# Routing and gates by tile 76, up- and down-projection fused from tile 80 on, every down-projection tile in three products

## The chip, the cores and the metric

One core of a Trainium2 chip runs the whole step. The metric is the device time of one execution in microseconds; the kernel before stands at a median of 1876.55 us over 3 runs (1875.07 to 1878.01). The clock of TensorE is told as a share of 2.4 GHz, of which the records of this case show two levels, 1.0 and 0.5.

## The reference, cut to what matters

One encoder layer: attention of two kinds, then PEER, a retrieval of single-neuron experts, added to the residual, then a norm. The change lies wholly within PEER, which reads per token 16 experts for each of 8 heads out of 16,384:

```python
q = (xb @ w_q).reshape(tb, PEER_HEADS, 2, D_KEY // 2)
s = jnp.einsum('thpc,pnc->thpn', q, sub_keys)
s_top, i_top = lax.top_k(s, PEER_TOPK)
cand_s = (s_top[:, :, 0, :, None] + s_top[:, :, 1, None, :])...
best_s, best_j = lax.top_k(cand_s, PEER_TOPK)
gate = jax.nn.softmax(best_s, axis=-1)
pre = jnp.einsum('thkd,td->thk', u[expert], xb)
act = jax.nn.gelu(pre) * gate
return jnp.einsum('thk,thkd->td', act, v[expert])
```

There are 576 tokens of width 1024: 512 of a prompt and 64 of a sample.

## The kernel before, in words

The first 600 us are projections and attention, which the change does not touch. PEER then treats the tokens in two ways. For 384 tokens (blocks D0, D1, D2) it computes all experts: 128 up-projection tiles ("U tiles") of 128 experts each, Gelu, a multiplication with a matrix of gates that is zero where an expert wasn't chosen, and 128 down-projection tiles ("V tiles"). For the other 192 tokens (blocks A with 128 and B with 64) GpSimd (POOL) gathers the chosen rows of u and v, 512 KB at a time, into a ring of buffers, 5 of them and 7 later on; VectorE (DVE) makes 192 dot products from rows of u and 192 weighted sums from rows of v. `OPS` is their order, and the table `DOT_LINE` tells how many DVE does beside each U tile.

**U tiles** (lines 974 to 992 on PE). Weights come as f32 by SP's queue into 4 buffers (`load_u`). ScalarE (ACT) rounds them to a high part, DVE subtracts it (`lo_part`, line 1339), and PE makes 3 products of rounded parts, 24 matmuls of 384 columns. ACT applies Gelu; the result of 112 tiles is stored to memory and loaded again, that of the last 16 (`KEPT`) stays.

**Routing and gates.** DVE finds the chosen experts beside the U tiles in small steps (`PLAN`, and `STEP_LINE` for how many per tile). From tile 64 on (`G_AT`), for 48 tiles, each has two groups of one-hot matrices (line 1718), which ACT scales and PE multiplies ("scatters", line 969); the gate matrix goes to memory.

**V tiles** (lines 994 to 1015). PE takes them in 128 places, `V_TILES` saying which tile stands at which place. Three places in four (`SPLIT`) are done as three products of rounded parts, 18 matmuls of 512 columns: ACT rounds p and v, DVE subtracts (`p_low`, `v_low`). Each fourth place is done in plain f32 (line 1012). Ahead of each place DVE multiplies the activations with the gates (`product`, line 1787), in the order `v_low(i+1)`, `product(i+3)`, `p_low(i+2)`, then some gathered sums.

**SP's queue in this stage** is written out by hand and waits in order. At place i it waits for V tile buffer i+6 to be free, that is for place i to be done (6 buffers), and asks for the next V tile; at some places it then asks for 4 tiles of activations; and it asks for gates, which come in groups of `GL_TILES` = 16 tiles, 2 buffers, each group in 4 pieces at i % 16 = 0, 3, 6, 9. DVE's product of a group's first tile waits for all 4 pieces.

## Time and profile before

| | |
|---|---|
| median of 3 runs | 1876.55 us |
| the profiled execution: its time, its span | 1875.91 us, 1874.1 us |
| PE busy | 1777.3 us, 95% |
| DVE busy | 1434.5 us, 77% |
| ACT, POOL busy | 778.4 us, 644.6 us |
| moved by DMA | 478.22 MB, 255 GB/s over the span |
| mean granted clock | 0.973 |

In this table PE looks like the one bound. It is an average over stages, and the stages are read in the windows and the chain further down. Matmul records overlap, since PE pipelines, so what a tile costs is read from the chain of waits, where starts follow each other; likewise DVE's records overlap by some 0.08 us, and its prices are read from start to start.

### The profile page before, as it was taken

To read this page: it belongs to the slowest core of one execution; us is meant where nothing else is said; L and a number is where in the kernel's file an instruction comes from. 1 tells how busy PE (TensorE), PEld (TensorE's weight loads), DVE (VectorE), ACT (ScalarE), POOL (GpSimd) and SP (SyncE) were. 2 spreads that over 40 slices of the span, in tenths; PEclk is the share of its full clock that TensorE was granted. 3 is DMA by queue.
4 is the path that set the end of the run, shared out by engine and by line. 5 is a ranking of instruction groups with operands and counts; after the bars stand their busy time and mean duration, and the time that the engine had idled before them with its cause. 6 is when DMAs were issued, how large, how long until landed. Compare 5 with 4: busy or idle time off the path is not lost.

```text
span 1874.1 us, 26361 instructions
## 1 busy us (share of the span) xinstructions
PE 1777.3 (95%) x9675; PEld 1516.0 (81%) x9675; DVE 1434.5 (77%) x2750; ACT 778.4 (42%) x1555; POOL 644.6 (34%) x409
## 2 busy tenths in 40 slices
PE   6999999989999899999999999978999999999997
PEld 6999776559998899999899999976676666766764
DVE  4433676665678788989999999867888788888787
ACT  3112566553444333333768788522222222222222
POOL 1100000000000133434223366555557566665672
PEclk8999799789999999999999999999999999999998
DMA  6233100002222589989788899999999999999996
GB/s 217 68 131 121 45 1 1 1 1 85 68 77 95 185 305 334 316 307 327 262 276 297 279 387 387 386 400 333 386 389 382 401 387 389 401 402 384 400 379 216
DMA packets 153599, 478.22 MB, mean 255 GB/s; under 512 B 14896, under 2 KB 53808, under 8 KB 149888
## 3 DMA queue, kind: packets, MB, share of 16 engines
q1 hardware_dynamic: 96112, 264.62, 38.7%
q0 software_dynamic: 56928, 208.28, 30.4%
q10 hardware_dynamic: 432, 3.64, 0.5%
q8 instruction: 77, 1.26, 0.3%
q14 instruction: 50, 0.41, 0.1%
HBM read 419.47 MB, written 56.75 MB: 254 GB/s over the span
## 4 chain that ended last, share of the span: by engine, by line
PE 69%; DVE 16%; DMA 8%; ACT 3%; issue 3%; POOL 0%; SPq 0%; ACTq 0%; DVEq 0%
PE ps L1003 17%; PE ps L981 16%; PE ps L633 10%; PE ps L1012 7%; PE ps L918 5%; DMA g_in<-gates_scattered 4%; PE ps L723 3%; DVE hot L1718 3%; DVE w_lo L1339 3%; DVE ring L1737 2%; PE ps L969 2%; PE ps L714 2%; PE ps L766 2%; DMA ring<-u_rows,idx_b 1%; DMA raw<-w_tiles 1%
## 5 line engine op out<-in xcount | busy, mean ns | idle before, releaser
L981 PE MATMUL ps<-md_hi,w_hi 128*128 128x384 f32 x1024 | 358.6, 350 | 36.9 <-DVE w_lo L1339 36.7
L981 PE MATMUL ps<-md_hi,w_lo 128*128 128x384 f32 x1024 | 345.8, 338 | 0.0
L981 PE MATMUL ps<-md_lo,w_hi 128*128 128x384 f32 x1024 | 345.7, 338 | 0.0
L613 POOL DMA_INDIRECT ring<-u_rows,idx_a x128 | 197.2, 1541 | 404.2 <-DVE dots L1737 294.8
L1339 DVE TENSOR_TENSOR w_lo<-raw,w_hi 128x1024 fp32r<-128x1024 f32 x176 | 215.3, 1223 | 79.2 <-ACT w_hi L1265 59.4
L613 POOL DMA_INDIRECT ring<-v_rows,idx_a x128 | 225.1, 1759 | 136.7 <-DVE acc L1747 105.4
L1737 DVE CUSTOM_DVE_ANT_0 ring<-ring,x_n 128x1024 f32<-128x1024 f32 x192 | 230.7, 1223 | 12.7 <-DMA ring<-u_rows,idx_b 10.7
L1747 DVE SCALAR_TENSOR_TENSOR acc<-ring,actg,acc 128x1024 f32<-128x1024 f32 x188 | 234.8, 1282 | 0.0
L981 PEld LDWEIGHTS ps<-md_hi,w_hi 128*128 128x128 f32 x1024 | 194.5, 190 | 46.3 <-DVE w_lo L1339 45.3
L1003 PE MATMUL ps<-w_hi,p_hi 128*128 128x512 f32 x576 | 193.0, 416 | 9.4 <-DVE w_lo L1805 9.1
L981 PEld LDWEIGHTS ps<-md_lo,w_hi 128*128 128x128 f32 x1024 | 194.5, 190 | 0.0
L981 PEld LDWEIGHTS ps<-md_hi,w_lo 128*128 128x128 f32 x1024 | 194.0, 189 | 0.0
L1003 PE MATMUL ps<-w_hi,p_lo 128*128 128x512 f32 x576 | 182.3, 397 | 0.0
L1308 ACT CAST w_hi<-v_buf 128x1024 fp32r<-128x1024 f32 x96 | 100.4, 1046 | 196.9 <-PE ps L1003 190.5
L1805 DVE TENSOR_TENSOR w_lo<-v_buf,w_hi 128x1024 fp32r<-128x1024 f32 x96 | 117.5, 1224 | 83.9 <-ACT w_hi L1308 83.7
L1003 PE MATMUL ps<-w_lo,p_hi 128*128 128x512 f32 x576 | 180.6, 395 | 0.0
L633 PE MATMUL ps<-m_hi,w_hi 128*128 128x296 f32 (+1 forms) x496 | 152.4, 307 | 14.6 <-DVE w_lo L1339 14.6
L1012 PE MATMUL ps<-v_buf,act_in 128*128 128x512 f32 x360 | 159.3, 592 | 0.0
L633 PE MATMUL ps<-m_hi,w_lo 128*128 128x296 f32 (+1 forms) x496 | 150.4, 303 | 0.0
L633 PE MATMUL ps<-m_lo,w_hi 128*128 128x296 f32 (+1 forms) x496 | 149.9, 302 | 0.0
L1003 PEld LDWEIGHTS ps<-w_hi,p_hi 128*128 128x128 f32 x576 | 108.1, 189 | 51.2 <-issue 27.6
L1265 ACT CAST w_hi<-raw 128x1024 fp32r<-128x1024 f32 x127 | 132.3, 1042 | 22.5 <-DMA raw<-w_tiles 22.4
(265 smaller groups left out, 3261.2 us busy)
## 6 DMA issues: line engine op xcount, KB each, us to landing
raw<-w_tiles SPq DMA_DIRECT2D x176, 512.0 KB, 5.2
v_buf<-v_rows SPq DMA_DIRECT2D x128, 512.0 KB, 11.4
gates_scattered<-g_st SPq DMA_DIRECT2D x24, 1024.0 KB, 6.7
g_in<-gates_scattered SPq DMA_DIRECT2D x32, 768.0 KB, 15.8
activated<-act_st SPq DMA_DIRECT2D x112, 192.0 KB, 4.2
act_in<-activated SPq DMA_DIRECT2D x28, 768.0 KB, 12.9
kv_t<-qkv ACTq DMA_DIRECT2D x3, 1184.0 KB, 4.7
xh<-x_t SPq DMA_DIRECT2D x8, 296.0 KB, 6.0
```

Of the source, the lines that this page charges most:

```text
L613: pool.indirect_dma_start(ring[slot][:], None, u_rows if table == "u" else v_rows, bass.IndirectOffsetOnAxis(ap=idx, axis=0)).then_inc(gat ...
L633: mm = nc.tensor.matmul(ps[:, 2 * slot + h, 0:width], w[:, slot, kc, :], x[:, kc, c0:c0 + width], start=(m == 0), stop=(m == 23))
L918: mm = nc.tensor.matmul(ps[:, 2 * slot + h, 0:HQ], w[:, slot, kc, :], x[:, kc, h * HQ:(h + 1) * HQ], start=(kc == 0 and j == 0), stop=(kc ...
L981: mm = nc.tensor.matmul(ps[:, slot, 0:ND], w[:, slot, kc, :], x[:, kc, :], start=(kc == 0 and j == 0), stop=(kc == KC - 1 and j == 2))
L1003: mm = nc.tensor.matmul(ps[:, 2 + 2 * t + h, :], p[:, q % 3, t * P:(t + 1) * P], v[q % 2][:, 512 * h:512 * h + 512], start=(i == 0 and n = ...
L1012: mm = nc.tensor.matmul(ps[:, 2 + 2 * t + h, :], acts(i)[:, t * P:(t + 1) * P], v_buf[i % V_SLOTS][:, 512 * h:512 * h + 512], start=False, ...
L1265: nc.scalar.copy(w_hi[:, n % 2], raw_u[k]).then_inc(hi_ready, 1)
L1308: nc.scalar.copy(v_hi[q % 2], v_buf[i % V_SLOTS][:]).then_inc(v_hi_ready, 1)
L1339: TT(w_lo[:, slot], raw[:, slot] if src is None else src, w_hi[:, slot].bitcast(F32), SUB).then_inc(w_split, 1)
L1737: nc.vector.tensor_tensor_reduce(rows, rows, x_n[:, blk], 1.0, 0.0, MULT, ADD, dots[:, blk, k:k + 1]).then_inc(gath_used, 1)
L1747: nc.vector.scalar_tensor_tensor(dst, rows, by, dst, MULT, ADD).then_inc(gath_used, 1)
L1805: TT(v_lo[q % 2], v_buf[i % V_SLOTS][:], v_hi[q % 2].bitcast(F32), SUB).then_inc(v_ready, 1)
```

## The change

1. **Routing earlier.** Blocks D0, D1, D2 are routed ahead of B (`PLAN`, with `RANK` for the count of finished blocks), all by tile 72. Gates are made beside tiles 28 to 75 (`G_AT` 28).
2. **Gathers moved.** `OP_LINE` takes the place of `DOT_LINE`: 25 gathered operations by tile 28, 45 by 76, 55 by 80, 252 by the end of U tile 127, the other 132 over the 80 V places behind. 16 sums of block A stand ahead of those of B.
3. **Fused part.** `FUSED` = 80: from U tile 81 on, each U tile is followed on PE by one V place, 47 places beside U tiles 81 to 127 and the rest behind ("the tail", places 47 to 127). The fused places take V tiles 80 to 127, whose activations stay on the core; 80 tiles are stored. The fused places have 4 buffers for V and one pair for its two parts (`vf_hi`, `vf_lo`), so the rounding of a V tile waits for the place before.
4. **Every V place split** (`SPLIT` is all 128).
5. **Gates in groups of 8 tiles**, pieces of 384 KB at j % 8 = 0, 2, 4, 6 instead of 768 KB at 0, 3, 6, 9 of 16.

The diff, cut to its core ("..." marks what is left out):

```diff
-PLAN = [("top", RT_A), ("sel", RT_B), ("top", RT_B), ("top", RT_D0), ("top", RT_D1), ("sel", RT_D2), ("top", RT_D2)]
+PLAN = [("top", RT_A), ("top", RT_D0), ("top", RT_D1), ("sel", RT_D2), ("top", RT_D2), ("sel", RT_B), ("top", RT_B)]
-STEP_LINE = [(0, 0), (7, 13), (64, 54), (90, N_STEPS)]
-G_AT = 64
+STEP_LINE = [(0, 0), (7, 13), (24, 26), (40, 39), (56, 57), (72, N_STEPS)]
+G_AT = 28
-GL_TILES = 16
-DOT_LINE = [(10, 0), (64, 67), (90, 97), (112, 140), (N_EXP, 178)]
+GL_TILES = 8
+FUSED = 80
+N_FUSED = N_EXP - FUSED
+V_TILES = [*range(FUSED, N_EXP), *range(FUSED)]
+OP_LINE = [(10, 0), (28, 25), (76, 45), (FUSED, 55), (N_EXP, 252), (N_EXP + FUSED, 384)]
...
-SPLIT = [i for i in range(N_EXP) if i % 4 != 3]
+SPLIT = list(range(N_EXP))
+V_SLOT, V_LAND, V_PREV = [], [], []
+for place in range(N_EXP):
+    slot = place % 4 if place < N_FUSED else (place - N_FUSED) % V_SLOTS
+    V_LAND.append(16 * (V_SLOT.count(slot) + 1))
+    V_PREV.append(max((p for p in range(place) if V_SLOT[p] == slot), default=None))
+    V_SLOT.append(slot)
...
+            def load_v(j):
+                slot, t = V_SLOT[j], V_TILES[j]
+                if V_PREV[j] is not None:
+                    sp.wait_ge(v_done, V_PREV[j] + 1)
...
+            def beside_place(j):
+                last = min(j + 3, N_FUSED - 1) if j < N_FUSED - 1 else min(j + V_SLOTS, N_EXP - 1)
+                while len(v_asked) <= last:
+                    load_v(len(v_asked))
+                    v_asked.append(j)
...
+                if j >= N_FUSED and j % 4 == 0:
+                    sp.wait_ge(v_done, j)
+                    g = (j - N_FUSED) // 4 + 2
+                    for g in range(1 if j == N_FUSED else g, min(g + 1, FUSED // 4)):
+                        load_acts(g)
+                if j >= 0 and j % 2 == 0 and 2 <= j // GL_TILES + 1 < N_EXP // GL_TILES:
+                    sp.wait_ge(p_made, j // GL_TILES * GL_TILES)
+                    load_gates(j // GL_TILES + 1, j % GL_TILES // 2)
...
-                if i % 16 in (0, 3, 6, 9) and i < N_EXP - 16:
-                    if i >= 16:
-                        sp.wait_ge(p_made, i // 16 * 16)
-                    load_gates(i // 16 + 1, i % 16 // 3)
+                if i > FUSED:
+                    beside_place(i - FUSED - 1)
+
+            for i in range(N_FUSED - 1, N_EXP):
+                beside_place(i)
...
+                if i == FUSED:
+                    pe.wait_ge(g_evac, N_GRP)
+                if i > FUSED:
+                    down(i - FUSED - 1)
+
+            for i in range(N_FUSED - 1, N_EXP):
+                down(i)
...
+                    q = SPLIT.index(i)
+                    act.wait_ge(v_in[V_SLOT[i]], V_LAND[i])
+                    before = q - (1 if i < N_FUSED else 2)
+                    if before >= 0 and (SPLIT[before] >= N_FUSED or i < N_FUSED):
+                        act.wait_ge(v_done, SPLIT[before] + 1)
...
             steps = routing()
             for i in range(N_EXP):
+                if i > FUSED:
+                    product(i - FUSED - 1)
...
+                if i > FUSED:
+                    p_low(i - FUSED - 1)
+                    v_low(i - FUSED - 1)
+                for s in ops_of(i):
                     gathered(s)
```

`down` holds the same 18 matmuls as the V loop before. In the tail DVE's order stays `v_low(i+1)`, `product(i+3)`, `p_low(i+2)`, sums.

How instructions stand on two engines, with the semaphores that they wait for (`v_done` counts finished places, `p_made` products, `g_in0` and `g_in1` landed gate pieces). First SP in the middle of the down-projection, before: the end of one group's pieces, with the requests for V tiles 90 to 95 (the last `g_in` row stands at place 89).

```order
L490 DMA v_buf_139<-v_rows 128x1024 [waits v_done]
L480 DMA act_in_147<-activated 128x1536 [waits v_done]
L490 DMA v_buf_140<-v_rows 128x1024 [waits v_done]
L490 DMA v_buf_141<-v_rows 128x1024 [waits v_done]
L475 DMA g_in_145<-gates_scattered 128x6x256 [waits p_made]
L490 DMA v_buf_142<-v_rows 128x1024 [waits v_done]
L490 DMA v_buf_143<-v_rows 128x1024 [waits v_done]
L480 DMA act_in_148<-activated 128x1536 [waits v_done]
L490 DMA v_buf_144<-v_rows 128x1024 [waits v_done]
L475 DMA g_in_145<-gates_scattered 128x6x256 [waits p_made]
```

After, in the tail, the end of a group of 8 (V tiles 87 to 92; the last `g_in` row stands at place 86, after the request for V tile 92).

```order
L507 DMA v_buf_144<-v_rows 128x1024 [waits v_done]
L507 DMA v_buf_145<-v_rows 128x1024 [waits v_done]
L491 DMA g_in_148<-gates_scattered 128x6x128 [waits p_made]
L507 DMA v_buf_146<-v_rows 128x1024 [waits v_done]
L507 DMA v_buf_141<-v_rows 128x1024 [waits v_done]
L496 DMA act_in_151<-activated 128x1536 [waits v_done]
L491 DMA g_in_148<-gates_scattered 128x6x128 [waits p_made]
L507 DMA v_buf_142<-v_rows 128x1024 [waits v_done]
L507 DMA v_buf_143<-v_rows 128x1024 [waits v_done]
L491 DMA g_in_148<-gates_scattered 128x6x128 [waits p_made]
```

Before, the last piece stands at place 89 and product 96 is the first that needs it; now it stands at place 86, and product 88 is the first that needs it.

DVE where a new group of gates begins, before: `act_in` rows are products, the one that waits for `g_in0` is product 96; there is no `p_lo` behind it for place 95, which is an f32 place.

```order
L1805 TENSOR_TENSOR w_lo<-v_buf_143,w_hi 128x1024 [waits v_done,v_hi_ready]
L1787 TENSOR_TENSOR act_in_148<-act_in_148,g_in_145 128x384 [waits act_in1,g_in0]
L1747 SCALAR_TENSOR_TENSOR acc<-ring_95,actg,acc 128x1024 [waits gath_used,gath_in2]
L1747 SCALAR_TENSOR_TENSOR acc<-ring_96,actg,acc 128x1024 [waits gath_used,gath_in3]
L1787 TENSOR_TENSOR act_in_148<-act_in_148,g_in_145 128x384
L1796 TENSOR_TENSOR p_lo<-act_in_148,p_hi 128x384 [waits v_done,p_hi_ready]
L1747 SCALAR_TENSOR_TENSOR acc<-ring_97,actg,acc 128x1024 [waits gath_used,gath_in4]
L1805 TENSOR_TENSOR w_lo<-v_buf_139,w_hi 128x1024 [waits v_done,v_hi_ready]
```

After, the same for product 88, which waits for `g_in1`; the `p_lo` behind it is that of place 87.

```order
L1794 SCALAR_TENSOR_TENSOR acc<-ring_97,actg,acc 128x1024 [waits gath_used,gath_in4]
L1801 TENSOR_TENSOR acc<-acc,b_half 64x1024 [waits b_sum,b_folded]
L1845 TENSOR_TENSOR w_lo<-v_buf_143,w_hi 128x1024 [waits v_done,v_hi_ready]
L1822 TENSOR_TENSOR act_in_150<-act_in_150,g_in_148 128x384 [waits act_in1,g_in1]
L1834 TENSOR_TENSOR p_lo<-act_in_149,p_hi 128x384 [waits v_done,p_hi_ready]
L1794 SCALAR_TENSOR_TENSOR acc<-ring_98,actg,acc 128x1024 [waits gath_used,gath_in5]
L1845 TENSOR_TENSOR w_lo<-v_buf_144,w_hi 128x1024 [waits v_done,v_hi_ready]
```

Between product 88 and `v_low` of place 87 (the last row) stand the remainder of place 87's p and one sum; PE's place 87 needs both remainders.

DVE in one iteration at the end of the U tiles, before (`dots` rows without a source finish the row ahead):

```order
L1339 TENSOR_TENSOR w_lo<-raw,w_hi 128x1024 [waits hi_ready]
L1737 ISA ring_97,dots<-ring_97,x_n 128x1024 [waits gath_in4]
L1737 ISA dots 128x1
L1737 ISA ring_93,dots<-ring_93,x_n 128x1024 [waits gath_in0]
L1737 ISA dots 128x1
L1339 TENSOR_TENSOR w_lo<-raw_100,w_hi 128x1024 [waits hi_ready]
```

After, one fused iteration:

```order
L1822 TENSOR_TENSOR act_in_150<-act_in_150,g_in_148 128x384 [waits act_done]
L1385 TENSOR_TENSOR w_lo<-raw_100,w_hi 128x1024 [waits hi_ready]
L1834 TENSOR_TENSOR p_lo<-act_in_150,p_hi 128x384 [waits v_done,p_hi_ready]
L1845 TENSOR_TENSOR vf_lo<-v_buf_141,vf_hi 128x1024 [waits v_done,v_hi_ready]
L1783 ISA ring_97,dots<-ring_97,x_n 128x1024 [waits gath_in4]
L1783 ISA dots 128x1
L1783 ISA ring_93,dots<-ring_93,x_n 128x1024 [waits gath_in0]
L1783 ISA dots 128x1
L1783 ISA ring_94,dots<-ring_94,x_n 128x1024 [waits gath_in1]
L1783 ISA dots 128x1
L1783 ISA ring_95,dots<-ring_95,x_n 128x1024 [waits gath_in2]
L1783 ISA dots 128x1
```

The product of a place, its two remainders and some four gathered operations now stand between two weight remainders of U tiles, where two or three gathered operations stood.

## Rows read from the trace of the kernel before

**Rows 1.** The page's slices, forty of the span: busy tenths of PE and DMA.
```profile
PE   6999999989999899999999999978999999999997
DMA  6233100002222589989788899999999999999996
```
**Rows 2.** Windows: stretch, length, busy us (instructions) of engines, PEclk, DMA share, GB/s.
```profile
888.00:1058.00 170.00, 160.15 (x1039) 157.05 (x1038) 165.53 (x317) 123.95 (x306) 52.94 (x31) 0.99 0.84 284
1058.00:1191.00 133.00, 129.80 (x864) 129.12 (x864) 128.21 (x160) 108.00 (x268) 77.21 (x43) 1.00 0.97 364
1191.00:1286.00 95.00, 77.09 (x431) 74.02 (x429) 69.56 (x102) 30.84 (x50) 52.48 (x41) 0.97 0.99 376
1286.00:1860.00 574.00, 570.88 (x2112) 398.35 (x2112) 463.70 (x542) 143.76 (x194) 347.11 (x202) 1.00 1.00 380
```
**Rows 3.** The chain that ended last: start us, us, what.
```profile
609.41 4.17 PE ps L981 x24
...
1097.85 2.63 PE ps L981 x15
1103.85 2.63 PE ps L981 x15
...
1306.17 12.56 PE ps L1003 x54
1318.73 5.15 PE ps L1012 x12
...
1860.40 3.68 DVE h_fin L1850 x6
```
**Rows 4.** DVE's timeline in the gate stage: start us, us, instruction.
```profile
1099.09 2.36 DVE L1718 TENSOR_TENSOR hot<-cst,rt_t 128x1024 f32<-128x1024 f32 x2
1101.36 1.23 DVE L1339 TENSOR_TENSOR w_lo<-raw,w_hi 128x1024 fp32r<-128x1024 f32 x1
1102.50 1.23 DVE L1737 CUSTOM_DVE_ANT_0 ring<-ring,x_n 128x1024 f32<-128x1024 f32 x1
1103.64 0.09 DVE L1737 DVE_READ_ACCUMULATOR2_ANT dots<- 128x1 f32 x1
```
**Rows 5.** DVE's timeline in the down-projection; in brackets idle time and its releaser.
```profile
1481.40 1.22 DVE L1805 TENSOR_TENSOR w_lo<-v_buf,w_hi 128x1024 fp32r<-128x1024 f32 x1
1482.54 0.55 DVE L1787 TENSOR_TENSOR act_in<-act_in,g_in 128x384 f32<-128x384 f32 x1
1483.01 0.55 DVE L1796 TENSOR_TENSOR p_lo<-act_in,p_hi 128x384 fp32r<-128x384 f32 x1
1483.48 2.47 DVE L1747 SCALAR_TENSOR_TENSOR acc<-ring,actg,acc 128x1024 f32<-128x1024 f32 x2
...
1494.91 0.56 DVE L1787 TENSOR_TENSOR act_in<-act_in,g_in 128x384 f32<-128x384 f32 x1 [5.19 <-DMA g_in<-gates_scattered]
```
**Rows 6.** Windows of line 981 alone, the U tiles: PE and weight loads, clock, DMA.
```profile
592.00:733.00 141.00, 119.93 (x659) 115.20 (x660) 0.99 0.73 250
```
**Rows 7.** Groups by line: ACT's rounding of a V tile.
```profile
L1308 ACT CAST w_hi<-v_buf 128x1024 fp32r<-128x1024 f32 x96 | 100.4, 1046 | 196.9 <-PE ps L1003 190.5 <-DMA v_buf<-v_rows 6.4
```
**Rows 8.** SP's timeline in the down-projection.
```profile
1473.84 0.33 SPq L490 DMA_DIRECT2D v_buf<-v_rows  x1
1474.22 0.43 SPq L475 DMA_DIRECT2D g_in<-gates_scattered  x1
```
**Rows 9.** DVE's waits from 1286 to 1860: us in total, times, longest.
```profile
DVE act_in L1787 <- DMA g_in<-gates_scattered: 26.0, 6, 6.0
```
**Rows 10.** PE's timeline at the first V tiles.
```profile
1285.88 1.19 PE L1003 MATMUL ps<-w_hi,p_hi 128*128 128x512 f32 x2 [6.28 <-DVE w_lo L1805]
...
1291.08 0.64 PE L1003 MATMUL ps<-w_hi,p_hi 128*128 128x512 f32 x2
```
**Rows 11.** The tile g_in: its loads of 768 KB.
```profile
DMA to landing us min/median/max: 7.6/15.8/21.5
```
**Rows 12.** The tile v_buf: its loads of 512 KB.
```profile
DMA to landing us min/median/max: 4.0/11.4/20.3
```

More of the change, by code:

```diff
@@ L525, in _ @@
                                  g_st[:, b % 2].rearrange("p i t -> p (i t)")).then_inc(g_stored[b % 2], 16)
+                if i == G_END + 1:
+                    for j in range(4):
+                        load_v(j)
+                        v_asked.append(j)
                 if i == G_END + 2:
@@ L971, in scatter, with down @@
                 mm.then_inc(hot_used, 1)
+            def down(i):
+                if i in SPLIT:
+                    q = SPLIT.index(i)
+                    hi, lo = v_parts(i)
+                    pe.wait_ge(p_ready, q + 1)
+                    pe.wait_ge(v_ready, q + 1)
+                    for t in range(3):
+                        for n, (p, v) in enumerate(((p_hi, hi), (p_hi, lo), (p_lo, hi))):
+                            for h in range(2):
+                                mm = nc.tensor.matmul(ps[:, 2 + 2 * t + h, :], p[:, q % 3, t * P:(t + 1) * P],
+                                                      v[:, 512 * h:512 * h + 512],
+                                                      start=(i == 0 and n == 0), stop=(i == N_EXP - 1 and n == 2))
+                    mm.then_inc(v_done, 1)
+                    return
+                pe.wait_ge(p_made, i + 1)
+                pe.wait_ge(v_in[V_SLOT[i]], V_LAND[i])
+                for t in range(3):
+                    for h in range(2):
+                        mm = nc.tensor.matmul(ps[:, 2 + 2 * t + h, :], acts(i)[:, t * P:(t + 1) * P],
+                                              v_buf[V_SLOT[i]][:, 512 * h:512 * h + 512],
+                                              start=False, stop=(i == N_EXP - 1))
+                mm.then_inc(v_done, 1)
             for i in range(N_EXP):
@@ L1741, in gathered @@
                 if s == N_U:
-                    dve.wait_ge(v_done, KEPT // 2)
+                    for stored in g_stored:
+                        dve.wait_ge(stored, 16 * (N_GB // 2))
                 if k < 2:
@@ L1802, in v_low @@
                     dve.wait_ge(v_hi_ready, q + 1)
-                    if q >= 2:
-                        dve.wait_ge(v_done, SPLIT[q - 2] + 1)
-                    TT(v_lo[q % 2], v_buf[i % V_SLOTS][:], v_hi[q % 2].bitcast(F32), SUB).then_inc(v_ready, 1)
-            product(0)
-            product(1)
-            product(2)
-            p_low(0)
-            v_low(0)
-            p_low(1)
-            for i in range(N_EXP):
+                    before = q - (1 if i < N_FUSED else 2)
+                    if before >= 0:
+                        dve.wait_ge(v_done, SPLIT[before] + 1)
+                    hi, lo = v_parts(i)
+                    TT(lo[:], v_buf[V_SLOT[i]][:], hi[:].bitcast(F32), SUB).then_inc(v_ready, 1)
+            steps = routing()
+            for i in range(N_EXP):
+                if i > FUSED:
+                    product(i - FUSED - 1)
+                for g in groups_of(i, 0):
+                    one_hot(g)
+                if i + 1 < N_EXP:
+                    lo_part(B_U + i + 1, (i + 1) % 2, raw_u[(i + 1) % RAW_SLOTS])
+                for s in range(5):
+                    if i == GATE_TILE[s] + 1:
+                        gates_of(s)
+                if i == OP_LINE[0][0] - 2:
+                    normed_rows()
+                for _ in range(along(STEP_LINE, i), along(STEP_LINE, i + 1)):
+                    s = next(steps)
+                    if s is not None:
+                        assert GATE_TILE[s] == i, (s, i)
+                        gates_below(s)
+                if i > FUSED:
+                    p_low(i - FUSED - 1)
+                    v_low(i - FUSED - 1)
+                for s in ops_of(i):
+                    gathered(s)
+            product(N_FUSED - 1)
+            p_low(N_FUSED - 1)
+            v_low(N_FUSED - 1)
+            for j in range(3):
+                product(N_FUSED + j)
+            p_low(N_FUSED)
+            v_low(N_FUSED)
+            p_low(N_FUSED + 1)
+            for i in range(N_FUSED, N_EXP):
                 if i + 1 < N_EXP:
@@ L1819, in _ @@
                     p_low(i + 2)
[L1820 removed]
+                for s in ops_of(N_EXP + i - N_FUSED):
                     gathered(s)
[L1822 to L1828 removed]
             n_fin = 0
```

242 lines of the change are left out of this document (98 added, 144 removed).

## The prediction, made blind

> **What bounds the kernel now.** First view, the page's slices [rows 1]: PE stands at 9 in most of the forty, and the DMA digits reach 9 for good in the 24th, at 1078 us. Two resources are full at once, so the stages have to be read one by one. The windows by stage [rows 2] show which: from 888 to 1191 us the stage of the gates, DMA share 0.84 and then 0.97; from 1191 to 1286 the last up-projection tiles, where PE is busy for only 77 of 95 us and the DMA share is 0.99; from 1286 to 1860 the down-projection, PE busy 571 of 574 us and a DMA share of 1.00 at 380 GB/s. PE sets the time nearly everywhere, and the DMA engines have nothing left after 1191.
>
> The chain of waits gives PE's prices [rows 3]: an up-projection tile is 4.17 us; with two scatters beside it the tiles come every 6.00 us (1097.85 to 1103.85); three split down-projection tiles take 12.56, so one 4.19; one tile in plain f32 takes 5.15; after PE's last product 14 us remain (1860.40 to the end of the span). DVE's prices are read from one start to the next [rows 4, 5]: 1.14 for a rounding remainder of a weight tile, 2.27 for a pair of one-hots, 1.14 for a gathered dot product, 1.2 for a gathered sum, 0.47 each for a product with the gates and its remainder.
>
> **The gate stage moves forward.** The gates now cover tiles 28 to 75 instead of 64 to 111. At 733 us PE has done 659/24 = 27.5 tiles [rows 6], with much the same mix of routing and gathers as the new order has there, so tile 28 begins near 735. The 48 tiles took 303 us before (888 to 1191), since 31 gathers and 20 routing steps beside the first 26 of them kept DVE busy 165.5 of 170 us [rows 2]. From that window a routing step is worth (165.5 - 26 x 3.41 - 31 x 1.14)/20 = 2.1 us. After: 48 x 3.41 + 20 gathers x 1.14 + 45 steps x 2.1 = 281 us of DVE under 48 x 6.00 = 288 us of PE. PE covers it, barely; I take 290, so 1025 us at tile 76. Then five plain tiles with 2.5 gathers each, and the first gate pieces and V tiles queued behind them: 4.5 us each (4.17 if PE alone counts), 1047 us.
>
> **Fused rounds, 47 of them (tiles 81 to 127 with places 0 to 46).** PE: 4.17 + 4.19 = 8.36 us. DVE: two remainders 2.28, product and its remainder 0.94, and 197 gathers over 48 rounds, 4.1 x 1.15 = 4.7; sum 7.9. DMA: 512 KB for the U tile, 512 KB for V, 4.1 x 512 KB of gathers, 192 KB of gates: 3.39 MB, at the 380 GB/s of the saturated stage 8.9 us. So DMA sets the round. Below it is bounded by PE, 8.36; above by the gather rate of the saturated stage with the same ring of 5 buffers, 41 gathers in 95 us [rows 2], 4.1 x 2.32 = 9.5. I take 9.1, near the bytes: 428 us, place 46 done at 1475 us (bounds 393 and 447).
>
> What hides the new single-buffered split of V (vf_hi, vf_lo): the rounding may begin only when the place before is done, and one U tile of 4.17 us lies between, against 1.05 on ACT [rows 7] and 1.14 on DVE.
>
> **All tiles split.** 32 tiles go from 5.15 to 4.19: 31 us less on PE. The 32 added remainders cost DVE 32 x 1.61 = 52 us, which fits: a tail place has 1.14 + 0.94 + 1.65 x 1.2 = 4.06 us of DVE under 4.19. Fewer stored activations (80 tiles for 112) take 12.6 MB off the queues.
>
> **Where the change adds a wait: the last gate piece of each group.** This decides the forecast. SP asks for V tile j+6 only when place j is done, since six buffers are all it has, and the gate pieces stand behind that request on the same queue. Before, the last of four pieces of a group of 16 goes out after place 9 of 16 and is wanted for place 16. The trace shows what this slack was worth: issue at 1474.22 [rows 8], wanted by DVE at 1489.7, used at 1494.91 after 5.19 us of waiting [rows 5]; six such waits, 26 us in all [rows 9]. PE had places 10 to 15 to do meanwhile, and place 15 was an f32 tile that needs no remainder. Now groups have 8 tiles, and the last piece goes out at place 8k+6, after that place is done. DVE meets product 8k+8 before the remainder of p for place 8k+7, so PE has nothing to do from the end of place 8k+6 until the piece has landed. Queued behind that product on DVE are the gathered sums too, whose buffers POOL needs for its next gathers; ACT's roundings of p for 8k+8 and of V for 8k+7 wait with it. The slack went from six places to none.
>
> Its price: 0.4 us for the V request and the issue ahead [rows 8]; the landing; then on DVE product 0.47, remainder 0.47, one or two gathered sums 2.0, remainder of V 1.14, with PE's own start about 4.2; and half speed afterwards. That last one is seen once: after 6.28 us of idling PE's records of two products last 1.19 us at 1285.88 and 0.64 from 1291.08 on [rows 10]; half of those 5.2 us is lost, 2.6. The landing of such a piece took 7.6 to 21.5 us at twice the size [rows 11], and a V tile 4.0 at best [rows 12]. The 15.8 of the median belongs to a queue without gaps. In the tail a group needs 8 x (512 + 1.65 x 512 + 192 of gates + 192 of activations) KB = 14.3 MB, 37.5 us at 380 GB/s, and the hole makes the group last longer than that, so the queue has run nearly dry when the piece goes out. I take 7 us, near the shortest row. A boundary costs 0.4 + 7 + 4.2 + 2.6 = 14.2 us; with a landing of 4 it is 11.2, with 12 it is 19.2.
>
> In the fused rounds the same piece has a U tile and a place more in front of it, and DVE comes to the product only 4.19 + 1.05 + 1.14 + 4.7 = 11 us after the issue (the place, the split of the next V tile, the gathers). There I charge nothing beyond the 9.1.
>
> **The sum**, against the profiled execution's 1875.91 us (span 1874.1; the median of the runs is 1876.55, so 0.6 above): place 46 at 1475, place 47 at 1479. Product 48 waits for a piece issued when U tile 127 was done, 1471, into a full queue: 1471 + 0.4 + 15.8 + 4.2 + 2.6 = 1494. Then 80 places x 4.19 = 335 and nine boundaries (products 56 to 120) x 14.2 = 128: 1957. With 14 at the end 1971, and 1.8 outside the span: **1972 us**. Seen as differences: 13 won in the gate stage, 26 where PE idled from 1191 to 1286, 31 from f32; lost 35 on fused rounds above PE's price and 143 at group boundaries.
>
> **Rivals.** (a) The other side: the gate piece is not waited for at the boundaries. That would hold if SP ran a few places ahead, or if a piece landed in the time that DVE has work; it decides where a boundary costs under (1876 - 1494 - 335 - 16)/9 = 3.4 us. Then the bytes set the tail: 80 x 4.69 = 375 us at 380 GB/s, 356 at 400: 1479 + 356 to 375 + 16 = 1851 to 1870, faster by 0.3 to 1.3%. For it: DVE's whole wait for gates was 26 us before. Against: the order of SP's and DVE's instructions, which leaves no place between. (b) Empty queues: the piece lands in about 4 us and a boundary costs 11.2; 1972 - 27 = 1945, and with rounds at PE's price 1910. For it: the hole itself empties the queues. (c) Rounds bound by the ring of 5 and boundaries with 12 us of landing: 1972 + 19 + 45 = 2036. For it: landings of 12 us and more are the rule once several requests are out. That the change doesn't do what it says is ruled out: the order shows the fused places and the split tiles.
> The shortest landing of a gate piece in the trace is 7.6 us for 768 KB [rows 11]. [...]
>
> **How the numbers follow.** Forecast 0.52, (b) 0.28, (c) 0.12, (a) 0.08. The range from 1900 to 2035 holds the forecast and (b) with the bounds of the rounds, and (c) but for its end; (a) lies outside. Chances, with 0.2% as about what a measurement of this kernel can tell from no change: faster 0.06, same 0.02 (both from (a)), slower 0.92.
>
> **What would show it.** After: gate stage near 6.0 us per tile from tile 28; rounds of 8.9 to 9.5 us with a DMA share near 1; then in the tail a PE gap of 9 to 15 us every eight places, ended by a wait of DVE for g_in, with half the granted clock behind it, and a DMA share falling to about 0.8. If those gaps are missing, the step on the last gate piece is wrong, and (a) holds. If the gaps are there but the rounds take over 10 us, the gather ring was mis-sized.

## The result: 2021.5 us, 7.8% slower, and the profile after

The changed kernel took 2021.53 us (median of four runs, 2015.98 to 2026.01) against 1875.81 for the kernel before, run beside it: a ratio of 1.0778, with a 95% interval from 1.0758 to 1.0798. The forecast was 1972 in a range from 1900 to 2035. The profiled execution took 2015.98 us with a span of 2014.2.

The page's slices of the changed kernel, to be laid beside [rows 1]. PE's nines end with the 30th slice, at 1511 us, in which the last U tile is done (1495.86); from there on PE and the DMA engines are both short of full, where before both were full.

```profile
PE   6999998899999989998995999999986776777756
PEclk9999798889999999999997999999998888888878
DMA  5243000012225887675779999999998888878885
```

The windows by stage, as in [rows 2]: stretch, length, busy us (instructions) of PE, weight loads, DVE, ACT and POOL, granted clock, DMA share, GB/s. They are the gate stage (tiles 28 to 75), the way to place 0, the fused rounds, the passage to places alone, and the tail with eight group boundaries.

```profile
748.00:1051.00 303.00, 292.06 (x1925) 287.52 (x1924) 271.05 (x545) 236.29 (x579) 34.52 (x21) 1.00 0.69 233
1051.00:1095.00 44.00, 23.10 (x124) 22.52 (x123) 23.02 (x33) 10.04 (x14) 16.25 (x14) 0.81 1.02 357
1095.00:1496.00 401.00, 388.64 (x1933) 349.62 (x1933) 371.75 (x507) 131.07 (x183) 256.30 (x188) 0.99 1.01 381
1496.00:1560.00 64.00, 41.68 (x163) 33.09 (x161) 36.19 (x43) 14.06 (x20) 22.00 (x16) 0.84 0.87 310
1560.00:1960.00 400.00, 279.69 (x1153) 227.16 (x1154) 264.85 (x302) 93.74 (x128) 184.55 (x107) 0.85 0.82 292
```

The tail is where the time went: PE works for 280 of 400 us. The waits of the whole span (us in total, times, longest) give the chain of causes: DVE waits for gate pieces where it waited 26.0 us before [rows 9], and PE waits for DVE's remainders behind that.

```profile
DVE act_in L1822 <- DMA g_in<-gates_scattered: 146.2, 10, 21.6
PE ps L1013 <- DVE w_lo L1845: 137.9, 12, 20.9
PE ps L1013 <- DVE vf_lo L1845: 33.9, 13, 16.8
```

One boundary in full, before place 87, from the timelines of SP, DVE and PE (start us, us, instruction, in brackets the idle time ahead and its releaser). They answer [rows 8], [rows 5] and [rows 10].

```profile
1745.59 0.33 SPq L507 DMA_DIRECT2D v_buf<-v_rows  x1
1745.97 0.43 SPq L491 DMA_DIRECT2D g_in<-gates_scattered  x1
...
1739.85 1.20 DVE L1845 TENSOR_TENSOR w_lo<-v_buf,w_hi 128x1024 fp32r<-128x1024 f32 x1
1754.95 0.56 DVE L1822 TENSOR_TENSOR act_in<-act_in,g_in 128x384 f32<-128x384 f32 x1 [13.90 <-DMA g_in<-gates_scattered]
1755.43 0.55 DVE L1834 TENSOR_TENSOR p_lo<-act_in,p_hi 128x384 fp32r<-128x384 f32 x1
1755.90 1.28 DVE L1794 SCALAR_TENSOR_TENSOR acc<-ring,actg,acc 128x1024 f32<-128x1024 f32 x1
1757.10 1.22 DVE L1845 TENSOR_TENSOR w_lo<-v_buf,w_hi 128x1024 fp32r<-128x1024 f32 x1
...
1744.95 0.61 PE L1013 MATMUL ps<-w_hi,p_lo 128*128 128x512 f32 x2
1758.46 1.19 PE L1013 MATMUL ps<-w_hi,p_hi 128*128 128x512 f32 x2 [12.90 <-DVE w_lo L1845]
1759.45 1.05 PE L1013 MATMUL ps<-w_lo,p_hi 128*128 128x512 f32 x2
...
1764.55 0.63 PE L1013 MATMUL ps<-w_lo,p_hi 128*128 128x512 f32 x2
```

This is the step of the prediction as it was drawn: the last matmuls of place 86 start at 1744.95, only then does SP ask for the next V tile and the last gate piece, DVE stands for 13.9 us, and PE starts 12.9 us later, for the first 6 us at a granted clock of 0.50 (two matmuls last 1.05 to 1.19 us instead of 0.62). There are nine such gaps, ahead of places 55, 63 and so on to 119, of 10.8 to 20.9 us.

The stretch around it in windows, 1720 to 1768, shows something that the prediction had wrong: the queue has not run dry when the last piece goes out. The DMA engines are full (share 1.03 and 1.04) at 1745.97 and for six us more. Cut to single us, their share is 1.09 from 1751 to 1752, then 0.64, 0.10 and 0.03; the piece lands at 1754.93. So they run empty only over the last 2 to 3 us of its way, and then idle while DVE and PE start again and have yet to free the buffers for new requests.

```profile
1720.00:1730.00 10.00, 10.00 (x45) 8.26 (x44) 10.00 (x12) 4.41 (x6) 8.01 (x4) 1.00 1.03 389
1730.00:1740.00 10.00, 10.00 (x46) 8.26 (x44) 10.00 (x12) 2.93 (x4) 6.40 (x6) 1.00 1.04 393
1740.00:1750.00 10.00, 4.73 (x20) 3.30 (x18) 1.05 (x1) 0.00 (x0) 1.88 (x1) 1.00 1.04 393
1750.00:1757.00 7.00, 0.00 (x0) 0.00 (x0) 2.04 (x3) 1.45 (x2) 0.00 (x0) 0.56 0.41 134
1757.00:1768.00 11.00, 9.54 (x30) 7.64 (x31) 9.88 (x12) 2.93 (x5) 8.05 (x5) 0.66 0.40 117
```

Counted over each of the eight groups from the packet records, the 14.2 to 16.5 MB of a group keep the 16 engines busy for 39 to 48 us, and they are idle for 9 to 12 (median 9.9) of its 49.95 us. So two things stand behind a group's time, PE's gap and the transfers, and the experiments had to tell how much belongs to each. (The packets' times overlap a little, which is why a share can be above 1.)

### The profile page after: what moved, and what is told of

Read it like the earlier page. It is cut to its first block, busy times and chain, and to the rows that moved or that the text cites. A ratio compares the mean times of both kernels' runs of the same rounds, so it can differ in the third digit from the quotient of the medians.

```text
span 2014.2 us, 27049 instructions
## 1 busy us (share of the span) xinstructions
PE 1760.2 (87%) x9867; PEld 1566.4 (78%) x9867; DVE 1491.8 (74%) x2814; ACT 821.0 (41%) x1619; POOL 598.6 (30%) x409
## 4 chain that ended last, share of the span: by engine, by line
PE 49%; DVE 23%; DMA 14%; issue 7%; ACT 3%; POOL 2%; SPq 2%; DVEq 0%; ACTq 0%
PE ps L1013 15%; PE ps L663 10%; PE ps L1035 7%; PE ps L948 5%; DMA g_in<-gates_scattered 4%; DVE w_lo L1385 3%; DVE ring L1783 3%; PE ps L753 3%; DMA ring<-u_rows,idx_b 3%; DMA ring<-u_rows,idx_a 3%; DVE acc L1794 3%; POOL ring L643 2%; DVE hot L1764 2%; PE ps L999 2%; PE ps L744 2%
## 5 line engine op out<-in xcount | busy, mean ns | idle before, releaser
L643 POOL DMA_INDIRECT ring<-u_rows,idx_a x128 | 180.8, 1412 | 504.9 <-DVE dots L1783 388.6
L1277 ACT CAST p_hi<-act_in 128x384 fp32r<-128x384 f32 x128 | 65.8, 514 | 571.1 <-DVE act_in L1822 398.7
L643 POOL DMA_INDIRECT ring<-v_rows,idx_a x128 | 218.4, 1707 | 231.1 <-DVE acc L1794 205.4
L1013 PE MATMUL ps<-w_hi,p_hi 128*128 128x512 f32 x480 | 158.1, 412 | 137.9 <-DVE w_lo L1845 137.9
L1013 PEld LDWEIGHTS ps<-w_hi,p_hi 128*128 128x128 f32 x480 | 94.5, 200 | 161.9 <-issue 142.6
L1822 DVE TENSOR_TENSOR act_in<-act_in,g_in 128x384 f32<-128x384 f32 x128 | 70.5, 552 | 153.7 <-DMA g_in<-gates_scattered 146.2
L1013 PE MATMUL ps<-w_lo,p_hi 128*128 128x512 f32 x480 | 154.3, 404 | 0.0
L1013 PE MATMUL ps<-w_hi,p_lo 128*128 128x512 f32 x480 | 153.4, 402 | 0.0
L1306 ACT ACTIVATE hot<-hot,rt_t 128x128 f32<-128x128 f32 x384 | 117.6, 391 | 28.3 <-DVE hot L1764 28.3
```

The costliest lines, as they stand in the source:

```text
L643: pool.indirect_dma_start(ring[slot][:], None, u_rows if table == "u" else v_rows, bass.IndirectOffsetOnAxis(ap=idx, axis=0)).then_inc(gat ...
L1013: mm = nc.tensor.matmul(ps[:, 2 + 2 * t + h, :], p[:, q % 3, t * P:(t + 1) * P], v[:, 512 * h:512 * h + 512], start=(i == 0 and n == 0), s ...
L1277: nc.scalar.copy(p_hi[:, q % 3], acts(i)).then_inc(p_hi_ready, 1)
L1306: last = nc.scalar.mul(h, h, rt_t[:, 2, 4 * g + t:4 * g + t + 1])
L1822: TT(p, p, g_in[grp % 2][:, :, V_TILES[i] % GL_TILES, :], MULT).then_inc(p_made, 1)
```

## The experiments

The ratios are to the kernel before, run beside each version (its medians were 1875.8 to 1879.7 us), with 95% intervals; medians in us.

| run | median | ratio | interval |
|---|---|---|---|
| changed kernel | 2021.5 | 1.0778 | 1.0758 to 1.0798 |
| last piece one place earlier | 2015.0 | 1.0737 | 1.0711 to 1.0763 |
| last piece three places earlier | 1956.5 | 1.0417 | 1.0393 to 1.0440 |
| product one place later on DVE | 2008.1 | 1.0689 | 1.0660 to 1.0717 |
| last piece seven places earlier | 1916.3 | 1.0184 | 1.0148 to 1.0220 |
| the same, fewer bytes | 1883.7 | 1.0012 | 0.9986 to 1.0038 |
| both starts | 2021.4 | 1.0759 | 1.0721 to 1.0797 |
| seven places earlier, both starts | 1908.5 | 1.0142 | 1.0108 to 1.0175 |
| long rows in the changed kernel | 2014.6 | 1.0728 | 1.0695 to 1.0761 |
| seven earlier, starts, long rows | 1892.1 | 1.0072 | 1.0046 to 1.0098 |
| before, all tiles split | 1887.3 | 1.0051 | 1.0031 to 1.0072 |
| before, long rows | 1869.7 | 0.9969 | 0.9950 to 0.9988 |
| before, all tiles split, long rows | 1863.5 | 0.9933 | 0.9913 to 0.9953 |

**The last gate piece one place earlier.** After the fused rounds, `at` names the places of a group behind which SP issues the four pieces ("..." marks what is left out):

```diff
-                if j >= 0 and j % 2 == 0 and 2 <= j // GL_TILES + 1 < N_EXP // GL_TILES:
...
+                at = (0, 2, 4, 6) if j < N_FUSED else (0, 2, 4, 5)
+                if j >= 0 and 2 <= j // GL_TILES + 1 < N_EXP // GL_TILES:
+                    for piece in range(4):
+                        if at[piece] == j % GL_TILES:
...
```

> The changed kernel with one line of SP's order altered: after the fused rounds the four gate pieces of a group go out after places 8k, 8k+2, 8k+4 and 8k+5, so the last one 4.1 us (one place) earlier than after place 8k+6. Theory (the wait at a group boundary is the time from the issue of the last piece to its landing): each of the nine PE gaps of 10.8 to 20.9 us gets shorter by one place, 4.1 us, and the stretch at half clock stays, since the gaps stay above 6 us: 9 x 4.1 = 37 us less than 2021, so about 1985. Rival (the DMA engines are at their limit in this stage and the late piece only shows it): a piece issued earlier lands as much later, the gaps stay, 2015 to 2022.

Measured: 2015.0, some 7 us less instead of 37. The intervals of the two ratios overlap, so the gain is at the edge of what can be told. The rows name the reason. The last piece ahead of place 87 goes out at 1742.57, and DVE goes on at 1755.16; in the changed kernel these stood at 1745.97 and 1754.95.

```profile
1738.11 0.33 SPq L507 DMA_DIRECT2D v_buf<-v_rows  x1
1738.48 0.50 SPq L496 DMA_DIRECT2D act_in<-activated  x1
1739.02 0.43 SPq L491 DMA_DIRECT2D g_in<-gates_scattered  x1
1742.19 0.33 SPq L507 DMA_DIRECT2D v_buf<-v_rows  x1
1742.57 0.44 SPq L491 DMA_DIRECT2D g_in<-gates_scattered  x1
...
1755.16 0.56 DVE L1826 TENSOR_TENSOR act_in<-act_in,g_in 128x384 f32<-128x384 f32 x1 [12.37 <-DMA g_in<-gates_scattered]
```

Its landing took 12.6 us instead of 9.0: the 768 KB of activations, the V tiles and the piece before were still in the queue. The two traces are shifted against each other; counted from the end of the gap before (1711.21 here, 1709.94 there) the piece was asked for 4.7 us earlier and DVE went on 1.1 us earlier, and a group takes 49.0 us for 49.95. So most of what the earlier issue won was lost again in the queue. Over one place the rival holds.

**Three places earlier.** `(0, 1, 2, 3)` in the same line.

> The same line altered further: pieces after places 8k, 8k+1, 8k+2 and 8k+3, the last one 12.3 us earlier than in the changed kernel. Theory: gaps of 10.8 to 16.8 us shrink to 0 to 4.5, too short for half clock behind them, so some 130 of the 149 us that the boundaries cost go, unless the bytes of the stage take over as the limit: a group of 8 places moves 14.3 MB, 37.5 us at the 380 GB/s of the old down-projection, so the 80 places could not take less than 375 instead of 487 us. Together 1885 to 1915. Rival (DMA at its limit already): 2000 to 2020, and a third story (the half clock comes from something else than the gaps) leaves the stretches at 0.500 in place, near 1960.

Measured: 1956.5, 65 us less, half of what the first theory gave and far more than the rival. The gaps are 2.1 to 11.3 us, half clock still behind most of them. The pieces land in 10.3 to 14.2 us in the stretch from 1741 to 1771, so part of the earlier issue is again eaten by the queue; but the queue now has work in time in which it was idle before (the DMA engines' idle time in a group is 4.4 us in the median for 9.9). Both stories were wrong by half. The third story named nearly this time, but not for its reason: of the eight gaps the seven of 7.4 us and more have half clock behind them, the one of 2.1 us has none, and in the version with the pieces seven places earlier, below, the long stretches at half clock go together with the gaps (granted clock 0.97). That gaps of up to 4.5 us would be too short for it is not borne out: in the changed kernel a gap of 4.75 us ahead of place 47 has 3.4 us at half clock behind it.

**The product one place later.** No transfer is moved; DVE makes the product two places ahead instead of three and the gathered sums ahead of the remainder of p, and ACT rounds V ahead of p, so place 87 no longer needs what stands behind product 88. DVE's part of the edit:

```diff
-                if i + 3 < N_EXP:
-                    product(i + 3)
-                if i + 2 < N_EXP:
-                    p_low(i + 2)
+                if N_EXP > i + 2 > N_FUSED + 2:
+                    product(i + 2)
                 for s in ops_of(N_EXP + i - N_FUSED):
                     gathered(s)
+                if i + 2 < N_EXP:
+                    p_low(i + 2)
```

> The changed kernel with no transfer issued at another time; after the fused rounds DVE makes the product with the gates two places ahead instead of three, behind the remainder of V of the next place, and ACT rounds V before p. So the first product of a group no longer stands ahead of what place 8k+7 needs, and PE has that place to do while the last gate piece is on its way. Theory: as much as one place's earlier issue, 4.1 us at each of nine boundaries, 37 in all: about 1985. Rival (the order of DVE's instructions doesn't matter, PE would wait for the same landing anyhow and the place is only moved to the other side of the gap; or the products made later delay the places in between): 2015 to 2030.

Measured: 2008.1, 13 us less, with intervals that don't touch. So the order on DVE is a part of the cause, as the prediction said; a group takes 48.6 us from the end of one gap to the end of the next (1567.9 to 1956.4, eight groups) instead of 49.95, 1.4 less where a place is 4.1. The DMA share stays at 0.84 and the pieces land later again, in 9 to 23 us.

**The theory after these three.** In a group of 8 places PE and the transfers each have work for less than the group takes, but each waits for the other once: the transfers' work (some 39 us) and the idle time that the boundary gives them (10 us) make up the group. An earlier issue can win the idle time and no more. That was put to the test with the piece seven places earlier, and with fewer bytes.

**Seven places earlier.** From the group of products 64 on, the pieces go out after places 8k-4 to 8k-1:

```diff
+  first = (g - 1) * GL_TILES
+  at = [first + 2 * n for n in range(4)] if first < N_FUSED else [
+      max(first - 4, N_FUSED) + n for n in range(4)]
...
```

> The changed kernel with the four gate pieces of a group issued after places 8k-4, 8k-3, 8k-2 and 8k-1 from the group of products 64 on (the group of 56 after places 48 to 51): the last one seven places, 28 us, earlier than in the changed kernel. Theory as now amended (PE's places and the transfers run one after the other: the DMA engines are at their full rate for 39 us of each group of 8 places and idle for 10 to 12 beside PE's gap; an earlier issue can win the idle time only): no wait for gate pieces is left, the group takes the 39 us that its 14.2 MB take at 370 to 380 GB/s, against 49.5 in the changed kernel and 43.2 with the last piece three places earlier: the time falls by 10 x 3.7 from 1956, to about 1920 (1905 to 1930), with a DMA share near 1. The prediction's own sum, with nothing but PE's 4.19 a place behind the gaps: 8 x 4.19 = 33.5 a group, 1956 - 97 = 1860. Rival (the queue holds what is asked for earlier just as long): 1950 to 1960.

Measured: 1916.3. DVE waits for no gate piece after the fused rounds, the gaps from place 55 to 119 are at most 4.0 us long, and what is left there is the transfers' limit. The window from place 55 to 119 of this kernel, to be laid beside the changed kernel's window from 1560 to 1960 above:

```profile
1558.00:1852.00 294.00, 273.26 (x1152) 219.75 (x1150) 262.92 (x298) 95.79 (x128) 190.22 (x105) 0.97 1.04 390
```

64 places in 294 us, 36.8 a group, DMA share 1.04, idle time of the DMA engines 0.0 in every group, 4.6 us a place where PE needs 4.1. The prediction's rival (a) had this price: 4.45 to 4.69 us a place once no piece is waited for.

**Fewer bytes.** The same with the loads of stored activations left out from the fourth group of four places on.

```diff
-                        load_acts(g)
+                        if g < 3:
+                            load_acts(g)
...
```

> The same with 17 of the 20 loads of stored activations left out, so the products from the fourth group of four places on are made from the wrong activations: a group of 8 places moves 12.6 MB instead of 14.2, 34.7 us of the DMA engines' time instead of 39. Theory (bytes set the places once no piece is late): 10 groups x 4.3 = about 40 us below the run with the early pieces, near 1880. Rival (PE, DVE or the order of the waits sets them): within 10 us of it.

Measured: 1883.7, 33 us less; a group takes 33.0 us (264/8), which is PE's 8 x 4.12.

```profile
1551.00:1815.00 264.00, 262.60 (x1155) 216.18 (x1154) 262.99 (x301) 94.00 (x129) 199.85 (x106) 1.00 1.04 385
```

So with all bytes the transfers set the places. With 11% fewer PE does, with 262.6 of 264 us busy, but only just: the DMA share is still 1.04. The loads left out also take their own waits away, but those were 5.6 us of DVE's in the version before, too little for the 33. The amended theory stands: 1920 and 1880 were expected.

**Both starts.** One V tile instead of four ahead of the first gate pieces, the pieces of group 1 after places 0, 2, 4 and 6, and another order of V buffers at place 48:

```diff
-    slot = place % 4 if place < N_FUSED else (place - N_FUSED) % V_SLOTS
+    slot = place % 4 if place < N_FUSED else (place - N_FUSED + 4) % V_SLOTS
...
-                    for j in range(4):
-                        load_v(j)
-                        v_asked.append(j)
+                    load_v(0)
+                    v_asked.append(0)
...
```

> The changed kernel with its group boundaries as they are, and the two starts mended: at tiles 77 to 79 SP asks for one V tile, the gate pieces of group 0 and one more V tile, the pieces of group 1 follow after places 0, 2, 4 and 6 (instead of four V tiles and both groups' pieces before place 0); and places 48 and 49 use the two V buffers that come free with the last U tile, not those of places 44 and 45. Theory: group 0's pieces had 1.5 MB of group 1's and 2 MB of V tiles in the queue beside them, and landed 17 to 24 us after their issue; without them the PE gap of 16.8 us before place 0 shrinks to 5 to 9 us, and the gap of 6.9 us before place 51 goes, with half clock behind each: 12 to 22 us less, 2000 to 2010. Rival (the gap before place 0 is the scattered gates' own way through memory, which no order changes): only the second, 2012 to 2016.

Measured: 2021.4 in the median, so nothing that can be told from no change, though its profiled execution took 2007.85. In the trace the gap ahead of place 0 is 11.4 us for 16.8, and the one ahead of place 51 is 4.1 for 6.9; with the early pieces beside it the latter is 7.0. The second half of the expectation is wrong. What DVE waits for ahead of place 51 is a group of activations (7.51 us in the changed kernel, 4.79 here): behind place 47 the changed kernel asks for four V tiles, two groups of activations and a gate piece within 7 us, 4.1 MB, and the order of the buffers makes them no fewer.

**Seven places earlier and both starts.**

> The early pieces and both starts together. Theory: the savings are at different places and add up, if the bytes leave room: 1920 less 12 to 22, about 1900 to 1908. If the stage after the fused rounds is set by its bytes, what the second start wins is given back there, and it is 1908 to 1915. Rival (the time lost at the starts is filled with transfers that then fail to stand in the queue later, so nothing is won): 1920.

Measured: 1908.5, on the border of the two ranges expected, but its interval overlaps that of the early pieces alone; whether the starts add anything stays open.

**Long rows.** The gates lie in DRAM by groups of 8 tiles, so a row of a piece has 3 KB instead of 512 bytes.

```diff
-    sp.dma_start(g_in[buf][:, b0:b0 + N_GB // 4].rearrange("p b i t -> p b (i t)"),
-                 g_dram[b0 * P:(b0 + N_GB // 4) * P, tiles * n:(tiles + 1) * n].rearrange(
-                     "(b p) n -> p b n", p=P)).then_inc(g_in_s[buf], 16)
+    sp.dma_start(g_in[buf][:, b0:b0 + N_GB // 4].rearrange("p b i t -> p (b i t)"),
+                 g_dram[tiles * P:(tiles + 1) * P, b0 * n:(b0 + N_GB // 4) * n]).then_inc(g_in_s[buf], 16)
...
```

> The changed kernel with one thing altered: the scattered gates lie in DRAM by groups of 8 tiles, so a gate piece has rows of 3 KB instead of 512 bytes (and the 24 stores of the gate stage have rows of 512 bytes instead of 8 KB). Theory (the transfers' time counts, and half a tile group per piece made it longer: 49152 packets of 512 bytes took 30 ns each in the changed kernel, 92 us over the 16 engines; the same bytes in 3 KB packets would take some 125 ns each by the rows of 1.5 and 4 KB, 64 us): 1.75 us less for each of 16 groups, of which the ten behind the fused rounds count in full since PE's work and the transfers follow one another there: 17 to 28 us less, 1993 to 2004. The stores' longer time is covered, since the DMA share of the gate stage is 0.68. Rival (the gaps are set by order alone, and the bytes are the same): 2016 to 2022.

Measured: 2014.6, 7 us less, where 17 to 28 were expected; the intervals of the two ratios overlap, so this too is at the edge of what can be told. The transfers did get shorter, by 1.3 to 2.5 us in each group, but the DMA engines' idle time grew from 10 to 11 us: as long as the gap is there, it is the order that sets it, and a shorter transfer is worth what it takes off the landing of the last piece (median of all pieces 8.5 us for 9.2).

> Early pieces, both starts and the long rows together. Theory: the stage behind the fused rounds is all transfer time now (idle time of the DMA engines 0.0 in each group), so the packets' 1.75 us a group come off in full there and in part in the fused rounds: 1908 less 17 to 28, 1880 to 1891, level with the kernel before or a little above it. Rival: PE or the waits set the places, 1903 to 1908.

Measured: 1892.1, 16 us less than without the long rows, with intervals that don't touch, and a microsecond above the expected range. Where the transfers set the places the shorter packets count. All parts of the changed kernel's loss that were tried are mended in this version, and it is still 0.7% slower than the kernel before. Its trace still has gaps of 10.3 us ahead of place 0, 5.0 us ahead of place 51 and 10.1 us near the end; what else it lacks stays open.

**The split alone, and the kernel before with long rows.** In the kernel before, one line (and the stop flag of the last place):

```diff
-SPLIT = [i for i in range(N_EXP) if i % 4 != 3]
+SPLIT = list(range(N_EXP))
```

> The kernel before with one part of the change alone: all 128 tiles of the down-projection as three products of rounded parts, instead of 96 of them. Theory of the prediction: PE is given back 32 x (5.15 - 4.19) = 31 us, and DVE's 52 us more fit beside it; if PE set the stage of 574 us alone that gives 1845. But the DMA share of that stage is 1.00, so the bytes set it nearly as tightly: then the gain is 0 to 12 us, 1864 to 1876, with PE gaps in place of the plain tiles. A third way: each group now lacks the plain tile that needed no remainder, so the wait for gate pieces reaches PE: slower by up to 20 us, 1895.

> The kernel before with the long rows alone (6 KB rows in a gate piece instead of 1 KB, stores with rows of 1 KB). Its gate pieces took 24576 x 48 ns / 16 = 74 us, by the packets of 6 KB (240 ns) it would be 61: 12 us of transfers less in a stage of 574 us whose DMA share is 1.00. But PE is busy there for 571 us: theory (both limits lie within a per cent of one another), 1870 to 1877. Rival (the bytes alone set that stage): 1865.

> The kernel before with two things: all tiles of the down-projection split, and the long rows. Theory (the split's 31 us were not to be had since the transfers set the stage; they come to light as far as the transfers get shorter): 12 us below the run with the split alone, 1887 - 12 = 1875, and some more where gaps with half clock behind them go: 1862 to 1875, below the kernel before. Rival (the split alone was slower because of the missing plain tile at each group's end, not because of the transfers): 1880 to 1887.

Measured: 1887.3, 1869.7 and 1863.5. The long rows alone are worth 0.3%, at the lower edge of the theory's 1870 to 1877. The split alone makes the kernel before 0.5% slower. PE's busy time falls (549 us, for 571 in [rows 2]), but the stage gets longer, from 574 to 584 us. Its gate pieces are waited for again, now by PE as well, with half clock behind: the third way of the expectation. The rows, of DVE and of PE:

```profile
1638.83 0.56 DVE L1787 TENSOR_TENSOR act_in<-act_in,g_in 128x384 f32<-128x384 f32 x1 [8.44 <-DMA g_in<-gates_scattered]
...
1643.53 1.20 PE L1003 MATMUL ps<-w_hi,p_hi 128*128 128x512 f32 x2 [7.64 <-DVE w_lo L1805]
```

The long rows bring the landing of a piece from 15.0 us in the median to 11.9 (15.8 in the kernel before [rows 11]), and with them the split wins: in the window of that stage PE is busy 541.6 of 554 us at a DMA share of 1.00.

```profile
1286.00:1840.00 554.00, 541.61 (x2303) 432.99 (x2301) 515.94 (x605) 186.25 (x255) 349.62 (x201) 0.99 1.00 394
```

That version is faster than both kernels, by 0.7% than the one before (0.9913 to 0.9953). The rival (the missing plain tile, not the transfers) falls in so far as the pieces now come in time without that tile.

## Why the prediction was right, step by step

The direction, the mechanism and its place were right, and the sum came out 50 us short (1972 for 2021.5; 44 against the profiled execution). In order of time:

- **Gate stage, 290 us for 48 tiles: wrong, 303.6.** ACT's Gelu of tile 28 is at 747.76 and that of tile 76 at 1051.40. The same 48 tiles took 303 before as well [rows 2]. The step priced a tile at the 6.00 us of one row of the chain [rows 3]; PE's busy time per tile in the stage is 292/48 = 6.08, and 0.2 of idling comes on top. DVE was not the limit (271 of 303 us), as said. With a start that lay some 9 us later than 735 (a Gelu comes a tile of PE after that tile's start), this is 22 us.
- **The way to place 0: a term that was missing, about 20 us.** PE idled 16.8 us ahead of place 0, with half clock behind. The first four gate pieces were issued at 1060.68 into a queue with four V tiles and U tiles ahead of them and landed after 10 to 24 us. The prediction had "the first gate pieces and V tiles queued behind them" and gave them 0.3 us a tile.
- **Rounds of 9.1 us: 8.72.** 46 of them from 1094.66 to 1495.86. The DMA share is 1.01, and the round lies inside its bounds (8.36 to 9.5), nearer to PE's price than the forecast. That gives 18 back. No product waits for gates there, as said.
- **Product 48 waits 15 us for its piece: it did not.** The piece landed in 5.7 us, and places 47 and 48 start at 1504.9 and 1510.68. That gives 8 back, after a gap of 4.75 us ahead of place 47 with half clock behind it. Ahead of place 51 stands a gap of 6.87 us instead: DVE waits 7.51 us for a group of activations that is asked for at 1515.33, behind four V tiles, and lands 9.9 us later. The sum had no term for it; with half clock it cost some 10.
- **A place, 4.19: 4.08.** Over 80 places 9 us less.
- **A boundary, 14.2 us, nine of them: 16.6, 149 for 128.** Taken apart at place 87: V request 0.4, landing from the issue on 9.0 (7 taken), DVE and PE's start 3.5 (4.2 taken), half clock 3.0, and 1.4 to 3.0 over the nine (2.6 taken). The landing was the size that was off: the nine last pieces took 6.8 to 14.6 us, 9.4 in the mean, and 2.4 us more at each of nine boundaries are the 21. Its reason was wrong: "the queue has run nearly dry when the piece goes out". It was full then, and at place 87 for six us more. The last boundary cost 22.4, since the five loads of h_fin are issued at place 116 and the piece behind them takes 14.6 us.
- **31 us from f32 on PE: right for PE, and worth nothing.** The split alone cost the kernel before 10 us; no run takes it out of the changed kernel. The stage before was bound by PE and by the transfers at once, which the first part of the prediction saw ("the DMA engines have nothing left after 1191"), and the sum then took PE's part as if it came off alone.
- **The tail's price behind the boundaries.** The sum had 4.19 a place, PE's. With the boundaries mended it is 4.6, the transfers' (rival (a)'s price), so removing the wait gave 105 us and not 149.

Four terms were too low, by 22, 20, 10 and 21 us, and three too high, by 18, 8 and 9. That is 38 of the 44 us; 2 more lie behind PE's last product (16 for 14), and some 4 stay unplaced. So the mechanism was right, but that the time fell into the stated range is in part luck: errors of opposite sign, in a range 135 us wide. The list of differences at the end of the prediction's sum doesn't close either: 70 won and 178 lost make 108, where 1972 less 1876 is 96.

Of the rivals, (b) with a landing of 4 us and (a) with none to wait for fall by the rows above; the pieces in the tail landed in 6.8 to 18.4 us. (c) came nearest in time, with 2036, but its rounds of 9.5 us were too long, and the mean landing of 9.4 lies halfway between the 7 of the forecast and its 12. The Trainium skill (DMA: Bandwidth & Descriptors, Anatomy of one DMA — SWDGE (gpsimd) path) fits 2.0 us plus the bytes at 436 GB/s to a transfer on GpSimd's path, by estimate 2.9 us for 384 KB. The pieces here go by SP's queue, and the shortest of 64 landings of 384 KB is 5.7 us, the median 9.2.

```profile
DMA to landing us min/median/max: 5.7/9.2/24.2
```

## What to carry to other kernels

Where two resources are full at once, take nothing off one of them as a gain before a look at what the other does with it: here 31 us of PE were worth minus 10 until the transfers had been made shorter as well. A load whose issue hangs on the consumer's own progress needs slack on both sides, and slack is counted in bytes that stand in the queue ahead of it: one place earlier was worth next to nothing, three won 65 us, seven ended the wait. Halving the groups of gates halved their rows in DRAM too; long rows were worth 16 us where the transfers set the places. Groups of 16 in the changed kernel were not tried.

## What was not expected of the hardware

- **Issuing a transfer can take 10 us.** SP's issue of a gate piece takes 0.43 us in the median; with nine of SP's transfers and three gathers out, one took 9.48, and with six and four the next took 9.67. Here are four pieces in SP's timeline, 23.59 us in all, with the next U tile queued behind:

```profile
1060.24 0.33 SPq L554 DMA_DIRECT2D activated<-act_st  x1
1060.68 23.59 SPq L491 DMA_DIRECT2D g_in<-gates_scattered  x4
1084.32 2.96 SPq L535 DMA_DIRECT2D raw<-w_tiles  x1
```

In the version with long rows and mended starts the same four took 1.77 us.

```profile
1065.04 1.77 SPq L491 DMA_DIRECT2D g_in<-gates_scattered  x4
```

The runs tell the two apart: with the mended starts alone, a shorter queue of short rows, the four took 14.00 us, one of them still 9.78; with long rows alone they took 4.18 us, though a piece of the second group then took 5.87. So here the rows counted for more than the length of the queue.

- **Packets of 512 bytes are dear.** From the packet records of the down-projection in the changed kernel, the one before and the one with all mended: 512 bytes take 29 ns on an engine (17.4 GB/s), 1 KB 48, 3 KB 126 (24.4 GB/s), 4 KB 166 to 174. The Trainium skill (DMA: Bandwidth & Descriptors, Specifications) gives 512 bytes as the least for line rate; here such packets ran more than a quarter below those of 3 KB, so the measurement speaks against it.
- **Half the granted clock stands behind short gaps too.** A gap of 3.77 us ahead of a place of the split-alone version has 3.4 us at 0.500 behind it; gaps of 11 to 14 us in the tail of the changed kernel go with 10 to 17 us at 0.500, the end of the gap among it.
